# Output-projection weights staged as bf16 in DRAM, and an attention bias table built first, in a whole-block kernel on eight cores

## The reference

```
hcat = x @ w_in                                # q, k, v of 8 dilated heads; u, v of the gates; q of 4 memory heads
o_dil = mixture over (window, dilation) in ((128,1), (512,4), (2048,16)) of windowed causal attention,
        logits + rel_bias[t5_bucket(distance)], merged by their softmax denominators
o_sg  = gelu(u) * (tril(w_spatial) @ layer_norm(gelu(v)) + b)      # in chunks of 128 tokens
o_mem = softmax(q_m k_m^T) v_m                                     # 256 memory tokens
mix = concat(o_dil, o_sg, o_mem) @ w_out
x = layer_norm(2**0.25 * x + mix)
f = (silu(x @ w_gate) * (x @ w_up)) @ w_down                       # width 5632
x = layer_norm(2**0.25 * x + f)
```

## Time and profile before

| | |
|---|---|
| median of 3 runs | 1659.28 us (1658.54 to 1661.97) |
| the profiled execution | 1660.26 us |
| its span on the slowest core, core 6 | 1658.4 us |
| spans of the 8 cores | 1635.6 to 1658.4 us |
| TensorE busy | 1607.6 us, 97% |
| VectorE, ScalarE, POOL busy | 485.3, 274.1, 95.3 us |
| casting DMAs (POOL) | 114.30 MB, 43.1% of the 16 engines' span |
| plain DMAs (SP) | 59.85 MB, 13.5% |

### The profile page before, as it was taken

How to read it: one execution, slowest core, us unless ns; L and a number is a source line. 1 busy time by engine, 2 the same in 40 slices (tenths; PEclk the granted TensorE clock), 3 DMA queues, 4 the chain that set the end, 5 groups by cost and what they waited for, 6 DMA issues and landing times.

```text
span 1658.4 us, 27518 instructions; the slowest of 8 cores (1635.6 to 1658.4 us)
## 1 busy us (share of the span) xinstructions
PE 1607.6 (97%) x11126; PEld 998.5 (60%) x11126; DVE 485.3 (29%) x737; ACT 274.1 (17%) x477; POOL 95.3 (6%) x135
## 2 busy tenths in 40 slices
PE   5999999999999996999999999999999999999997
PEld 2788877455555552444444444444444478888996
DVE  0063100166666673981111111111111101120248
ACT  0110111254444430341000000000000000000000
POOL 3100000000000000000010010000000000001000
PEclk9999999999999997999999999999999999999998
DMA  9999663225434897455466484444444254444443
GB/s 142 154 172 175 125 108 76 44 50 93 79 70 76 141 177 167 164 153 109 77 109 114 77 146 77 77 76 77 77 76 77 50 204 71 71 71 75 87 128 153
DMA packets 138470, 175.90 MB, mean 106 GB/s; under 512 B 54467, under 2 KB 85443, under 8 KB 136812
## 3 DMA queue, kind: packets, MB, share of 16 engines
q0 software_dynamic: 63024, 114.30, 43.1%
q1 hardware_dynamic: 75324, 59.85, 13.5%
HBM read 265.31 MB, written 23.11 MB: 174 GB/s over the span
## 4 chain that ended last, share of the span: by engine, by line
PE 86%; DMA 7%; SPq 4%; DVE 1%; issue 1%; POOL 1%; ACT 0%; DVEq 0%; ACTq 0%; POOLq 0%
PE psf L354 63%; PE psf L1168 19%; SPq L290 4%; DMA ring<-winsg 3%; DMA woc<-wout 2%; DMA trilf<-tril 2%; POOL xTo L287 0%; PE psf L1050 0%; PE psf L709 0%; PE psf L710 0%; PE psf L732 0%; PE psf L734 0%; PE psf L733 0%; PE psf L735 0%; DVE vg L365 0%
## 5 line engine op out<-in xcount | busy, mean ns | idle before, releaser
L354 PE MATMUL psf<-x1T,gu 128*128 128x512 bf16 x2816 | 608.4, 379 | 0.4 <-ACT sgt L1077 0.4
L354 PEld LDWEIGHTS psf<-x1T,gu 128*128 128x128 bf16 x2816 | 275.3, 98 | 332.2 <-issue 0.8
L1080 DVE TENSOR_TENSOR hTa<-psf,sgt 128x512 bf16<-128x512 f32 x64 | 44.3, 692 | 386.3 <-PE psf L354 376.4
L354 PE MATMUL psf<-xTo,ring 128*128 128x512 bf16 x640 | 153.3, 379 | 0.0
L1077 ACT ACTIVATE sgt<-psf 128x512 f32<-128x512 f32 x88 | 52.5, 597 | 532.8 <-PE psf L354 530.9
L354 PE MATMUL psf<-xTh,ring 128*128 128x512 bf16 x512 | 126.8, 379 | 0.0
L1168 PE MATMUL psf<-wdB,hTa 128*128 128x256 bf16 x1024 | 117.0, 273 | 0.0
L354 PE MATMUL psf<-ring,xTh 128*128 128x256 bf16 x1024 | 112.3, 273 | 0.0
L354 PEld LDWEIGHTS psf<-ring,xTh 128*128 128x128 bf16 x1024 | 100.2, 98 | 11.8
L1168 PEld LDWEIGHTS psf<-wdB,hTa 128*128 128x128 bf16 x1024 | 99.8, 98 | 11.4
L354 PE MATMUL psf<-woc,ocatT 128*128 128x512 bf16 x384 | 88.6, 391 | 14.2 <-DMA woc<-wout 14.2
(11 more groups left out here) (158 smaller groups left out, 1419.6 us busy)
## 6 DMA issues: line engine op xcount, KB each, us to landing
gu<-wgu POOLq DMA_DIRECT2D x44, 1024.0 KB, 8.9
wdB<-wd POOLq DMA_DIRECT2D x16, 704.0 KB, 12.4
wdA<-wd POOLq DMA_DIRECT2D x12, 704.0 KB, 12.4
xTh<-xTh POOLq DMA_DIRECT2D x8, 1024.0 KB, 52.7
ring<-winqk POOLq DMA_DIRECT2D x8, 1024.0 KB, 12.2
woc<-wout POOLq DMA_DIRECT2D x8, 1024.0 KB, 17.3
Y<-x1d SPq DMA_DIRECT2D x8, 1024.0 KB, 10.0
vd<-vst SPq DMA_DIRECT2D x96, 64.0 KB, 8.5
```

Source lines behind the costliest of these rows:

```text
L354: return [(lambda e, ps, k=k: e.matmul(ps, lhsT=lhs(k), rhs=rhs(k), start=(k == 0), stop=(k == n - 1))) for k in range(n)]
L1080: S.op("dve", lambda e: e.tensor_tensor(out=hT_ap(f_, slice(tb * 512, (tb + 1) * 512)), in0=ps, in1=sgt[tb][:, :], op=ALU.mult), reads=[bn ...
```

## The change

Three edits, the numbers of lines shift by one to two.

- The loads of `relx` and `ohs` get a group of their own (semaphore `s_c6`) without a wait, at the very start of SP's list; the three bias matmuls with VectorE's copies and the store of `gtab` follow at once, so they stand at the very start of TensorE's and VectorE's lists too. They go from their old place after `vg`.
- A DRAM tensor `wob` in bf16 for the output weights, filled by eight casting DMAs from DRAM to DRAM on POOL (`stage_wo`): pieces 0 and 1 in head 0, 2 and 3 in head 1, and one in each of heads 2 to 5, behind `load_qk`.
- The eight loads of `woc` read `wob` and no longer cast. They stay on POOL, at the same places.

```diff
+        S.dma("sp", [plain_dma(relx[0:32, :], d_rel.ap()),
+                     plain_dma(ohs[:, :, :], d_oh.ap().rearrange("p (r u) -> p r u", u=384))], "s_c6", writes=["relx", "ohs"])
+        S.op("dve", lambda e: e.memset(relx[32:33, :], -30000.0), writes=["relx32"])
...
+        for r in range(3):
+            b = nextbank()
+            S.op("pe", lambda e, b=b, r=r: e.matmul(psf[b][:, 0:384], lhsT=relrep[:, :, :].rearrange("p a h -> p (a h)"),
+                                                  rhs=ohs[:, r, :], start=True, stop=True),
+                 reads=["relrep", "ohs"], writes=[f"ps{b}"])
...
-        S.dma("sp", [plain_dma(relx[0:32, :], d_rel.ap()),
-                     plain_dma(ohs[:, :, :], d_oh.ap().rearrange("p (r u) -> p r u", u=384)),
-                     plain_dma(identf[:, :], d_ident.ap()),
+        S.dma("sp", [plain_dma(identf[:, :], d_ident.ap()),
                      plain_dma(validf[:, :], d_valid.ap())],
-              "s_c0", after=["ring3"], writes=["identf", "validf", "relx", "ohs"])
+              "s_c0", after=["ring3"], writes=["identf", "validf"])
...
+        def stage_wo(i, after):
+            c, k0, k1 = i // 2, 8 * (i % 2), 8 * (i % 2) + 8
+            S.dma("pool", cast_dma(d_wob.ap()[c][:, 512 * k0:512 * k1], d_wout.ap()[c][:, 512 * k0:512 * k1]),
+                  f"s_wob{i}", after=after, writes=[f"wob{i}"])
+
+        def wo_part(c, i):
+            return lambda e: e.dma_start(out=woc[c][:, 8 * i:8 * i + 8, :],
+                                         in_=d_wob.ap()[c].rearrange("p (k c) -> p k c", c=512)[:, 8 * i:8 * i + 8, :])
...
         def load_wo(c, after=()):
-            S.dma("pool", [cast_dma(woc[c][:, 8 * i:8 * i + 8, :],
-                                    d_wout.ap()[c].rearrange("p (k c) -> p k c", c=512)[:, 8 * i:8 * i + 8, :]) for i in range(2)],
-                  f"s_wo{c}", after=after, writes=[f"wo{c}"])
+            S.dma("pool", [wo_part(c, i) for i in range(2)], f"s_wo{c}", reads=[f"wob{2 * c}", f"wob{2 * c + 1}"],
+                  after=after, writes=[f"wo{c}"])
...
             if h <= 5:
                 load_qk(h + 2)
+                for i in ((2 * h, 2 * h + 1) if h < 2 else (h + 2,)):
+                    stage_wo(i, ["Vt4", "T4", "Vt16", "T16h"])
```

More of the change, by code:

```diff
@@ L184, in build_program @@
     d_vd = nc.dram_tensor("vd", [4, 3072 * 256], BF16)
+    d_wob = nc.dram_tensor("wob", [4, 128, 16 * 512], BF16)
     d_x1 = nc.dram_tensor("x1d", [1024, 2048], F32)
@@ L372, in norm_b @@
                  reads=list(names) + [mn, "ln_b"], writes=out_names)
+        S.dma("sp", [plain_dma(relx[0:32, :], d_rel.ap()),
+                     plain_dma(ohs[:, :, :], d_oh.ap().rearrange("p (r u) -> p r u", u=384))], "s_c6", writes=["relx", "ohs"])
+        S.op("dve", lambda e: e.memset(relx[32:33, :], -30000.0), writes=["relx32"])
+        S.op("dve", lambda e: e.tensor_copy(out=relrep[:, :, :], in_=relx[:, :].unsqueeze(1).broadcast_to([33, 16, 8])),
+             reads=["relx", "relx32"], writes=["relrep"])
+        for r in range(3):
[3 more added lines that the diff above has]
+                 reads=["relrep", "ohs"], writes=[f"ps{b}"])
+            S.op("dve", lambda e, b=b, r=r: e.tensor_copy(out=gsb[:, r, :], in_=psf[b][:, 0:384]),
+                 reads=[f"ps{b}"], writes=["gsb"])
+        S.dma("sp", plain_dma(bass.AP(d_g, 0, [[3 * GROW, 8], [GROW, 3], [1, GROW]]), gsb[0:8, :, :]), "s_g",
+              reads=["gsb"], writes=["g"])
         KA0 = [range(0, 4), range(4, 8)] + [range(2 * i, 2 * i + 2) for i in range(4, 8)]
@@ L445, in build_program @@
         S.op("dve", lambda e: e.memset(eps[:, :], LN_EPS), writes=["eps"])
-        S.op("dve", lambda e: e.memset(relx[32:33, :], -30000.0), writes=["relx32"])
         S.op("dve", lambda e: e.tensor_copy(out=identb[:, :], in_=identf[:, :]), reads=["identf"], writes=["identb"])
@@ L449, in build_program @@
              reads=["validf"], writes=["vones"])
-        S.op("dve", lambda e: e.tensor_copy(out=relrep[:, :, :], in_=relx[:, :].unsqueeze(1).broadcast_to([33, 16, 8])),
-             reads=["relx", "relx32"], writes=["relrep"])
         def load_xTh(tb):
@@ L484, in build_program @@
         run_all([vg_group(1, t) for t in range(8)])
[L485 to L493, removed]
         S.alias(["ohs", "relx", "relx32", "relrep", "gsb", "identf"], ["xTh0"])
@@ L867, in build_program @@
         OCA = [f"oc{k}_{tb}" for k in range(8, 16) for tb in range(2)] + [f"oc{k}" for k in range(7)]
+        def stage_wo(i, after):
[5 more added lines that the diff above has]
+                                         in_=d_wob.ap()[c].rearrange("p (k c) -> p k c", c=512)[:, 8 * i:8 * i + 8, :])
         def load_wo_half(i, after=()):
-            S.dma("pool", cast_dma(woc[3][:, 8 * i:8 * i + 8, :],
-                                   d_wout.ap()[3].rearrange("p (k c) -> p k c", c=512)[:, 8 * i:8 * i + 8, :]),
-                  f"s_wo3{i}", after=after, writes=[f"wo3{i}"])
+            S.dma("pool", wo_part(3, i), f"s_wo3{i}", reads=[f"wob{6 + i}"], after=after, writes=[f"wo3{i}"])
         def load_wo(c, after=()):
-            S.dma("pool", [cast_dma(woc[c][:, 8 * i:8 * i + 8, :],
-                                    d_wout.ap()[c].rearrange("p (k c) -> p k c", c=512)[:, 8 * i:8 * i + 8, :]) for i in range(2)],
-                  f"s_wo{c}", after=after, writes=[f"wo{c}"])
+            S.dma("pool", [wo_part(c, i) for i in range(2)], f"s_wo{c}", reads=[f"wob{2 * c}", f"wob{2 * c + 1}"],
+                  after=after, writes=[f"wo{c}"])
         def wo0_group(t):
```

## The result

The changed kernel takes **1650.52 us**, the median of 11 runs; 11 runs of the kernel before on the same chip have a median of 1661.05 us. The ratio is **0.9934, 95% interval 0.9923 to 0.9945**: 10.5 us faster, where 19.3 were forecast, and half a microsecond above the range.

A forecast was written before the change was run, and what follows sets the result against it. The prediction saw a chain of TensorE matmuls, with the slowest core, 6, waiting on DMAs. Its terms -18.45 - 0.9 + 2.0 - 2.0 = -19.35 took the span from 1658.4 to 1639.05, forecast 1640 us, range 1635 to 1650.

The forecast's parts named there:

- Part 1: Output projection after head 7: plain loads of the output weights end TensorE's waits for woc, 18.45 us gained.
- Part 2: Staging DMAs in heads 0 to 5: their only cost is DMA contention, mainly head 1's wait for Vt, +2.0 us.
- Head 1 now has the same 3 MB: there at 361.67 + 30.4: Head 1's Vt loads: there at 392.1, wanted at 391.2, so 0.9 us late, reckoned from head 6 before.
- f: Factor by which a staged MB takes longer than 6.6 us; head 1 waits 0.9 + 13.2(f - 1).
- rival A: Staging takes more, f from 1.3 to 2: head 1 waits 5 to 14 us; 1645.5, up to 1656; chance 0.15.
- signs named beforehand: If right: head 1's Vt loads about 24 us, head 6's under 18, cores' spans within some 5 us, no woc wait.
- Part 3: Bias table at the start: trilf lands earlier in the opening by 2.4 us less 0.4, taken as -2.0 us.
- rival D: Start: first TensorE work waits for the table's loads and ends 3 to 5 us late; 1644; chance 0.05.
- What is late next: Part 1's check after the output projection: VectorE's ln1b would be 0.4 us late; nothing counted.
- E: After the output projection: ln1b lands 8 us later, VectorE carries some 5 us to the end; 1645; chance 0.08.
- C: Output weights: a plain load from DRAM lands no sooner than a casting one; 1659.3; chance 0.04.
- B: Staging makes the kernel slower than before, with waits in heads 2 to 5 too; 1675.5 at f = 2.5; chance 0.04.

The follow-up runs named there:

- experiment 6: Kernel before plus eight DRAM-to-DRAM DMAs copying bf16 without a cast, same bytes written, output weights still loaded with a cast: 1.0013 of the kernel before.
- experiment 5: Kernel before plus the eight casting staging DMAs alone, their copy read by nobody: 1.0031 of the kernel before, +5.1 us.
- Experiments 7: Changed kernel with the staging of heads 1 to 5 issued behind the same head's Vt loads: 1639.84 us, 0.9906 of the kernel before.
- 12: Changed kernel with the staging of heads 1 to 5 behind the same head's Vt loads, run again on another chip: 1639.57 us, 0.9913 of the kernel before.
- experiments 1: Kernel before with only the bias table moved to the start: 0.9989 of the kernel before, -1.8 us.
- 2: Changed kernel with the bias table at its old place, output weights staged and loaded plain: 0.9954 of the kernel before.
- experiment 3: Changed kernel with three pieces staged in head 0 and one each in heads 1 to 5: 0.9927 of the kernel before.
- 4: Changed kernel with the 2 MB load of xTh2 moved behind the load of the fourth winv piece: 0.993 of the kernel before.
- 9: Changed kernel with staging of heads 1 to 5 behind the same head's Vt loads and xTh2 behind the fourth winv piece: 1637.77 us, 0.9901 of the kernel before.
- 10: Changed kernel with staging behind Vt loads, xTh2 behind the fourth winv piece, and bias table at its old place: 1639.81 us, 0.9915 of the kernel before.
- 8: Changed kernel with six pieces staged in the quiet stretch before head 0 and two in head 0: 1649.59 us, 0.9962 of the kernel before.
- 11: Changed kernel as it is, run again on another chip: 1646.91 us, 0.9955 of the kernel before.

## Why the prediction was wrong

**Part 1, right in mechanism and size.** 18.45 us forecast for the output projection, 18.46 measured between the same two matmuls, no wait for `woc` on any core. The steps hold one by one: head 6's `Vt` loads under 18 us (6.65), head 7's under 13.5 (5.39), the `wo2` issue at 602 (600.28, with a head 1 that lasted 8.7 us longer). Plain loads of 1 MB land 9.2 us after their issue in the median on core 6, the casting ones 17.3. The loads changed in two ways, no cast and rows in one piece of 4096 elements, and no run separates the two. The reading that 328 GB/s was the most over several microseconds was wrong: it is 434 (experiment 6, last row). Nothing hung on it, for the chunks were early anyway.

**Part 2, the step that failed.** "Head 1 now has the same 3 MB: there at 361.67 + 30.4": it equated a staged MB with a casting load of head 6. The rows put it at f = 156 / 120 = 1.3 (written rates in head 6 before and head 1 after), and the engine time of experiment 5, 8.7 to 9.3 us against 6.6, at 1.3 to 1.4. My own formula then gives 0.9 + 13.2 x 0.3 = 4.9 us of wait, against 5.67 on core 6 and 3.6 to 6.0 on the five cores that stall. So the lever was right and f was taken too low: the row of head 6 was the nearest, but it is a DMA that doesn't write DRAM. By the figure of the Trainium skill's page HBM Reference, section Specifications (TRN2), which the prediction worked out and set aside, a staged MB takes 8.8 us and head 1 waits 5.3; the trace agrees in heads 0 and 1, and not in heads 2 and 3 with 6.0 us. Second, the term left out what the stall costs afterwards. 3.0 us of matmuls at the lower clock follow, which the earlier trace rows showed (15 matmuls in 5.73 us where they take 3.40) and which I had used for the gain but not for the loss. 2.0 forecast, 8.7 measured on core 6, and 5.1 (2.6 to 7.6) on the whole kernel in experiment 5. That is rival A in kind, at its lower end. Experiments 7 and 12 show what decided it: the staging stood ahead of head 1's `Vt` loads, and behind them it costs no wait. Two of the signs named beforehand pointed the same way: head 1's `Vt` loads took 28.12 us, not 24, and the cores' spans are 13.3 us apart, not 5.

**Part 3, right in what it moves; what it brought is open.** `trilf` comes 1.9 us earlier (experiments 1 and 2; 2.4 less 0.4 forecast), and the table's matmuls are hidden; rival D fell, with 11 us in hand. "What is late next" wasn't asked: the fourth `winv` piece landed at 125.9 on core 6 before and was wanted at 126.9, 1 us in hand. In the changed kernel seven of the eight cores wait 1.9 to 3.7 us for it, so part of the gain is eaten; how much, the totals don't tell. With it out of the way the table is worth 2.0 us, as forecast.

**Not in the sum:** 2.1 us for `wdB` in the last stage of core 6. I didn't trace it. A wait of 0.2 to 2.9 us for it is also there on some cores in experiments 3, 4, 6, 7, 9, 10 and 12, of which 6 loads its output weights as before; in 2, 8 and 11, which have the change, there is none. E fell: nothing waits for `ln1b`. C fell with part 1. B fell: heads 2 to 5 have no wait on any core.

**Sum** on core 6 (output projection, staging, opening, heads 2 to 7, the end): -18.5, +8.7, -1.3, -1.2, +2.4 in place of -18.45, +2.0, -2.0, -0.9, 0. They differ by about 9.4 us, of which 6.7 are the staging.

What stays open: why the stall takes one core of most pairs (0 and 1, 2 and 3, 4 and 5, 6 and 7) and mostly spares the other. It is other cores in other runs, and mostly those that were also late in the opening. Two cores that share a memory would give such a picture, but nothing here separates them. Open too is why a staged MB takes 9 us of the engines in heads 0 and 1, where two are issued together, and 6 in heads 2 and 3.

## What to carry to other kernels

Traffic moved off a critical stage costs where it lands. Price it by its own kind: here a cast from DRAM to DRAM took two to three times the engine time of a plain load of the same size (6.0 to 9.3 us against 3.2). Where it lands, look for the small loads queued behind it rather than for quiet bytes: the same eight DMAs cost 7.3 us more ahead of a head's small loads than behind them, and a quiet stretch was as bad a place, because the next stage's small loads were in it. And when a stage is shortened, list what has less in hand than the gain; here a landing had 1 us in hand where 2 were to be gained.

## What the runs showed of the hardware

- SP's issue of small loads can take very long while large DMAs fill the engines: a table load 22.69 us with six staged MB issued ahead of it (0.3 elsewhere), three `Vt4` loads 13.61 us with three (1.90 in the kernel before). A full DMA share alone doesn't do it: `relx` took 0.40 us at 60.00, at a share of 1.09 from 60 to 66.
- Written GB/s in stretches of 5 to 25 us at a DMA share of 0.9 to 1.1: 328 to 434 for plain loads, 149 to 165 for casts into SBUF, 110 to 158 in head 1 with casts from DRAM to DRAM in flight. The share alone tells none of them apart.
- Engine time of a DMA of 1.05 MB from DRAM to DRAM (estimates, experiments 5 and 6): 8.7 to 9.3 us with a cast and 4.3 to 5.5 without, where two are issued together; 6.0 and 3.8 for one.
- A stall of 5.7 us of TensorE brought 3.0 us more at a granted clock of 0.50; the 0.87 us of the earlier trace rows and the 1.93 us of experiment 3 brought none that shows.
